# Expert sums, end norm, third norm and the second half's first products in one stage, tile by tile

## The reference, cut to what matters

```python
    h = h + hier_moe(rms_norm(h, norm2_gain[l]), ...)   # each token: two experts' rows, weighted
    return rms_norm(h, final_norm_gain)                 # "end norm"; result is x of the second half

    h = rms_norm_2(x, norm_mix_pre[l])                  # "third norm"
    c_q, c_kv, k_rope, sc_b, sc_c, sc_h, ssd_in = jnp.split(h @ w_in[l], IN_SPLITS, axis=-1)
    ...
    x = x + rms_norm_2(mixed, norm_mix_post[l])         # x is needed again here
```

## Time and profile before

| | us |
|---|---|
| median of 3 runs | 3203.65 |
| lowest and highest of them | 3199.31 and 3207.77 |
| the profiled execution, whole | 3191.12 |
| its span, first to last instruction | 3189.4 |

### The profile page before, as it was taken

The page is one execution under the profiler, slowest core; times in us unless marked ns, Lnnn a source line. Parts: engine busy times, 40 slices in busy tenths (PEclk is TensorE's granted clock), DMA queues, the critical chain, the costliest instruction groups (busy, mean ns, idle before and its releaser), DMA issues. The chain is left out here.

```text
span 3189.4 us, 39300 instructions
## 1 busy us (share of the span) xinstructions
PE 2807.9 (88%) x14664; PEld 2310.0 (72%) x14665; DVE 1757.9 (55%) x2227; ACT 1342.4 (42%) x1915; POOL 405.5 (13%) x387
## 2 busy tenths in 40 slices
PE   7999799989967299999993699679989999998997
PEld 6988577777856078888882588457768888887886
DVE  4441276777643389999995412766665334433313
ACT  4111255555531077777873423334444323322212
POOL 0000064556510200000002000220000000000000
PEclk9999899999978699999996799889999999999998
DMA  7543200010051589999984201000041111110113
GB/s 252 194 174 126 103 27 33 33 65 25 8 171 60 175 328 412 408 411 407 405 365 185 75 27 39 18 1 1 0 161 52 46 46 52 46 46 27 50 49 140
DMA packets 173926, 418.23 MB, mean 131 GB/s; under 512 B 28604, under 2 KB 116592, under 8 KB 160496
## 3 DMA queue, kind: packets, MB, share of 16 engines
q1 hardware_dynamic: 158688, 362.59, 30.7%
q0 software_dynamic: 9360, 33.04, 2.6%
q10 hardware_dynamic: 5760, 20.97, 1.6%
HBM read 347.85 MB, written 68.72 MB: 131 GB/s over the span
## 5 line engine op out<-in xcount | busy, mean ns | idle before, releaser
L134 PE MATMUL psum<-part,ffn_up_w_high 128*128 128x512 f32 x704 | 277.8, 395 | 0.7 <-DVE low L3357 0.7
L136 PE MATMUL psum<-part,ffn_up_w_low 128*128 128x512 f32 x704 | 276.1, 392 | 0.0
L135 PE MATMUL psum<-low,ffn_up_w_high 128*128 128x512 f32 x704 | 273.5, 389 | 0.0
L3371 DVE SCALAR_TENSOR_TENSOR ffn_up_acc<-psum,ffn_up_taps,ffn_up_acc 128x1023 f32<-128x1023 f32 x88 | 112.8, 1282 | 285.4 <-ACT ffn_up_acc L3292 279.6
L134 PE MATMUL psum<-part,expert_x_high 128*128 128x512 f32 x512 | 206.6, 403 | 2.9 <-issue 1.5
L134 PE MATMUL psum<-project_w_high,high 128*128 128x448 f32 (+1 forms) x512 | 196.8, 384 | 13.0 <-DVE project_w_low L129 9.0
L136 PE MATMUL psum<-part,expert_x_low 128*128 128x512 f32 x512 | 203.4, 397 | 0.0
L135 PE MATMUL psum<-project_w_low,high 128*128 128x448 f32 (+1 forms) x512 | 195.4, 382 | 0.0
L136 PE MATMUL psum<-project_w_high,low 128*128 128x448 f32 (+1 forms) x512 | 195.3, 381 | 0.0
L3292 ACT ACTIVATE ffn_up_acc<-psum,ffn_up_taps 128x1024 f32<-128x1024 f32 x44 | 53.2, 1208 | 333.9 <-PE psum L136 333.9
L1080 POOL TENSOR_TENSOR mix_ab_step<-mix_abrb,mix_pair_mask 128x512 f32<-128x512 f32 x80 | 115.1, 1463 | 420.9 <-ACT mix_abrb L1193 420.5
(11 more groups left out here) (575 smaller groups left out, 6957.5 us busy)
## 6 DMA issues: line engine op xcount, KB each, us to landing
expert_gate<-in_w_gate_dram SPq DMA_DIRECT2D x32, 2048.0 KB, 10.0
expert_up<-in_w_up_dram SPq DMA_DIRECT2D x32, 2048.0 KB, 10.0
expert_down<-in_w_down_dram SPq DMA_DIRECT2D x32, 2048.0 KB, 10.8
ffn_up_w<-in_ffn_w_up_dram SPq DMA_DIRECT2D x44, 512.0 KB, 3.8
y_rows<-expert_y ACTq DMA_DIRECT2D x32, 512.0 KB, 10.8
ffn_down_w<-in_ffn_w_down_dram SPq DMA_DIRECT2D x44, 256.0 KB, 2.6
project_w<-in_w_in_dram SPq DMA_DIRECT2D x4, 2048.0 KB, 10.3
ret_feat<-project_out SPq DMA_DIRECT2D x4, 2048.0 KB, 10.1
```

The costliest lines, as they stand in the source:

```text
L134: pe.matmul(out, left[0], right[0], start=start, stop=False)
L135: pe.matmul(out, left[0], right[1], start=False, stop=False)
L136: return pe.matmul(out, left[1], right[0], start=False, stop=stop)
L3371: v.scalar_tensor_tensor(out=acc[c][u][:, i:], in0=wide(psum, 4 * u + 2 * c, 2)[:, 0:S - i], scalar=taps[:, last_tap - i, ds(at, 1)], in1= ...
```

## The change

`combine_stage` and `norm_stage` go, and `project2_stage` takes in their work. Tile `t` is gathered, summed, multiplied by the end gain (`weighed`), squared twice (the sum, and the weighed sum), scaled once by both norms' factors and both gains (`xs`), turned, split and multiplied. The factors of both norms come from one chain of small operations on two numbers a row (`means`, `root`, `scale`). POOL makes the rows of `x2_rows` (weighed rows by the end norm's factor), and SP stores them. The gathers have two buffers in place of eight, the products three pairs of banks in place of four, the other pair takes the transposes. The gain of the third norm is now a row (a multiplication on DVE before the transpose), so the high part and the rest are each written in two pieces of 128 x 512. The first two loads of `w_fm` and their splits stand apart from the loop.

```diff
-                combine_stage(nc, x, squares, y_rows, slot_index, slot_weight, a["final_norm_gain"], x2_dram)
-            norm_stage(nc, "norm3", bank, ident, x, squares, a["norm_mix_pre_2"], part, low=low)
+        def tm_bank(t, n):
+            return bank[2 * (t % 3) + n]
...
+            gather(0)
+            gather(1)
+            for t in range(TT):
+                if t + 2 < TT:
+                    pool.wait_ge(summed, 2 * t + 2)
+                    gather(t + 2)
+                pool.wait_ge(xs_ready, t + 1)
+                pool.tensor_scalar(weighed[t % 2][:], weighed[t % 2][:], x_stats[:, t, 3, 0:1], None, ALU.mult).then_inc(x_ready, 1)
         @block.sync
+            sp.dma_start(end_gain[:], rows(a["final_norm_gain"], D)).then_inc(end_gain_loaded, 16)
+            sp.dma_start(gain[:], rows(a["norm_mix_pre_2"], D)).then_inc(gain_loaded, 16)
...
+            for u, at in enumerate((SC_AT, XBC_AT)):
+                load_fm(0, u, at)
+            for t in range(TT):
+                sp.wait_ge(x_ready, t + 1)
+                sp.dma_start(x_dram[t * P:(t + 1) * P, :], weighed[t % 2][:]).then_inc(x_stored[t % 2], 16)
         @block.tensor
+            turn(0)
             for t in range(TT):
-                tile = slice(t * P, (t + 1) * P)
-                if t >= 4:
-                    pe.wait_ge(latent_out, t - 3)
-                    pe.wait_ge(z_out, t - 3)
+                pe.wait_ge(feat_low_out, 2 * t + 2)
+                if t >= 3:
+                    pe.wait_ge(latent_out, t - 2)
+                    pe.wait_ge(z_out, t - 2)
                 for n, (lo_, hi) in enumerate(((0, LATENT), (LATENT, TM_COLS))):
+                    if n and t + 1 < TT:
+                        turn(t + 1)
...
         @block.scalar
+            def square_sum(t):
+                act.wait_ge(summed, 2 * t + 2)
+                if t:
+                    act.wait_ge(squared, 2 * t)
+                act.activation(acc[:], x[:, t, :], ACT.Square, accum_out=x_stats[:, t, 0, 0:1]).then_inc(squared, 1)
...
+            def take_high(t):
+                act.wait_ge(turned, t + 1)
+                for h in range(2):
+                    split_high(act, tile(high, t)[:, 4 * h:4 * h + 4, :], three(bank[6 + h][:], 4)).then_inc(feat_high_out, 1)
...
+            split_tm(0)
+            square_sum(0)
+            square_weighed(0)
+            split_tm(1)
+            root(0)
+            split_tm(2)
+            split_tm(3)
+            take_high(0)
+            square_sum(1)
+            square_weighed(1)
+            split_tm(PIECES)
+            root(1)
+            for t in range(TT):
+                if t + 2 < TT:
+                    square_sum(t + 2)
+                if t + 1 < TT:
+                    take_high(t + 1)
+                if t + 2 < TT:
+                    square_weighed(t + 2)
+                take_latent(t)
+                if t + 2 < TT:
+                    root(t + 2)
+                if t == TT - 3:
+                    for u in range(2):
+                        split(0, u)
...
         @block.vector
+            def add(t):
+                v.wait_ge(gathered[t % 2], t // 2 * 32 + 32)
+                for c in range(2):
+                    if c:
+                        v.wait_ge(summed, 2 * t + 1)
+                    v.scalar_tensor_tensor(out=x[:, t, :], in0=got[t % 2][:, c, :], scalar=slot_weight[:, c, t:t + 1],
+                                           in1=x[:, t, :], op0=ALU.mult, op1=ALU.add).then_inc(summed, 1)
+            def weigh(t):
+                v.wait_ge(summed, 2 * t + 2)
+                if t >= 2:
+                    v.wait_ge(x_stored[t % 2], t // 2 * 16)
+                v.tensor_tensor(weighed[t % 2][:], x[:, t, :], end_gain[:], ALU.mult).then_inc(weighed_ready, 1)
+            def means(t):
+                v.wait_ge(squared, 2 * t + 2)
+                v.tensor_scalar(x_stats[:, t, 1, 0:1], x_stats[:, t, 0, 0:1], 1.0 / D, EPS, ALU.mult, ALU.add).then_inc(stats_order, 1)
+                v.wait_ge(stats_order, t * 4 + 1)
+                v.reciprocal(x_stats[:, t, 3, 0:1], x_stats[:, t, 1, 0:1]).then_inc(stats_order, 1)
+                v.wait_ge(stats_order, t * 4 + 2)
+                v.tensor_tensor(x_stats[:, t, 3, 1:2], x_stats[:, t, 0, 1:2], x_stats[:, t, 3, 0:1], ALU.mult).then_inc(stats_order, 1)
+                v.wait_ge(stats_order, t * 4 + 3)
+                v.tensor_scalar(x_stats[:, t, 1, 1:2], x_stats[:, t, 3, 1:2], 1.0 / D, EPS, ALU.mult, ALU.add).then_inc(mean_ready, 1)
+            def scale(t):
+                v.wait_ge(root_ready, t + 1)
+                v.reciprocal(x_stats[:, t, 3, :], x_stats[:, t, 2, :]).then_inc(stats_order, 1)
+                v.wait_ge(stats_order, t * 4 + 4)
+                v.tensor_tensor(x_stats[:, t, 2, 0:1], x_stats[:, t, 3, 0:1], x_stats[:, t, 3, 1:2], ALU.mult).then_inc(both_ready, 1)
+                v.wait_ge(both_ready, t + 1)
+                if t >= 2:
+                    v.wait_ge(turned, t - 1)
+                v.scalar_tensor_tensor(out=xs[t % 2][:], in0=weighed[t % 2][:], scalar=x_stats[:, t, 2, 0:1], in1=gain[:],
+                                       op0=ALU.mult, op1=ALU.mult).then_inc(xs_ready, 1)
+            def take_low(t):
+                for h in range(2):
+                    v.wait_ge(feat_high_out, 2 * t + h + 1)
+                    split_low(v, tile(low, t)[:, 4 * h:4 * h + 4, :], three(bank[6 + h][:], 4), tile(high, t)[:, 4 * h:4 * h + 4, :])\
+                        .then_inc(feat_low_out, 1)
...
+            add(0)
+            v.wait_ge(end_gain_loaded, 16)
+            weigh(0)
+            split_tm(0)
+            means(0)
+            split_tm(1)
+            v.wait_ge(gain_loaded, 16)
+            scale(0)
+            add(1)
+            weigh(1)
+            split_tm(2)
+            split_tm(3)
+            take_low(0)
+            means(1)
+            split_tm(PIECES)
+            scale(1)
             for t in range(TT):
-                v.wait_ge(product, 2 * t + 2)
-                v.tensor_copy(rows2[:, t, LATENT:], bank[2 * (t % 4) + 1][:, 0:SSD + SSD_HEADS]).then_inc(z_out, 1)
+                if t + 2 < TT:
+                    add(t + 2)
+                    weigh(t + 2)
+                if t + 1 < TT:
+                    take_low(t + 1)
+                if t + 2 < TT:
+                    means(t + 2)
+                take_z(t)
+                if t + 2 < TT:
+                    scale(t + 2)
+                if t == TT - 3:
+                    for u in range(2):
+                        split(0, u)
```

More of the change, by code:

```diff
@@ L143, in square_rows @@
     act.activation(junk[t % 2][:], x[:, t, :], ACT.Square, accum_out=squares[:, t:t + 1]).then_inc(done, 1)
[L146 to L240, removed]
@@ L2265, in _ @@
             each_more(v, more_block)
[L2268 to L2316, removed]
-                    v.scalar_tensor_tensor(out=x[:, t, :], in0=x[:, t, :], scalar=rstd[:, t:t + 1], in1=gain[:], op0=ALU.mult,
-                                           op1=ALU.mult).then_inc(normed, 1)
-        @block.scalar
-        def _(act):
-            for g in range(TT // GROUP):
-                for t in range(g * GROUP, (g + 1) * GROUP):
-                    act.wait_ge(added, 2 * t + 2)
-                    if t >= 2:
-                        act.wait_ge(squared, t - 1)
-                    act.activation(junk[t % 2][:], x[:, t, :], ACT.Square, accum_out=square[:, t:t + 1]).then_inc(squared, 1)
-                act.wait_ge(mean_ready, g + 1)
-                act.activation(root[:, g * GROUP:(g + 1) * GROUP], mean[:, g * GROUP:(g + 1) * GROUP], ACT.Sqrt).then_inc(root_ready, 1)
-            act.wait_ge(squared, TT)
-            for t in range(TT):
-                act.wait_ge(normed, t + 1)
-                square_rows(act, x, t, junk, squares, x_squared)
@@ L2462, in scale_first, with split_tm, square_weighed, root @@
                     .then_inc(sc_scaled, 1)
-            for n, (ks, ns) in enumerate(tm_parts):
+            def split_tm(n):
+                ks, ns = tm_parts[n]
                 act.wait_ge(tm_loaded[n], 32 if n == PIECES else 16)
                 split_high(act, w_tm_high[:, ks, ns], w_tm[:, ks, ns]).then_inc(tm_high_ready, 1)
-            for u in range(2):
-                split(0, u)
-            for t in range(TT):
+            def square_sum(t):
[3 more added lines that the diff above has]
+                act.activation(acc[:], x[:, t, :], ACT.Square, accum_out=x_stats[:, t, 0, 0:1]).then_inc(squared, 1)
+            def square_weighed(t):
+                act.wait_ge(weighed_ready, t + 1)
+                act.wait_ge(squared, 2 * t + 1)
+                act.activation(acc[:], weighed[t % 2][:], ACT.Square, accum_out=x_stats[:, t, 0, 1:2]).then_inc(squared, 1)
+            def root(t):
+                act.wait_ge(mean_ready, t + 1)
+                act.activation(x_stats[:, t, 2, :], x_stats[:, t, 1, :], ACT.Sqrt).then_inc(root_ready, 1)
```

(15 more changed lines are left out.)

57 lines of the change are left out of this document (43 added, 14 removed).

## The result

| | before | after |
|---|---|---|
| median | 3201.48 us (4 runs, 3190.55 to 3207.77) | 3154.67 us (4 runs, 3149.01 to 3165.87) |
| span of the profiled execution | 3189.4 | 3158.4 |
| the stage (see below) | 147.4 | 102.6 |

The ratio is 0.9862, with a 95% interval from 0.9819 to 0.9904: 46.8 us less on the medians, where 46 were forecast.

A forecast was written before the change was run, and what follows sets the result against it. Vector engines and DMA bound the first part, PE the rest, one behind the other. Overlapped, start, 9.5 us periods and PE's tail end at 1814.1 instead of 1861.0: 46.9 saved, rounded to 46, giving 3157.7 us, range 3143 to 3180.

The forecast's parts named there:

- The bound before, and the form of the gain: Experts' end to loop of 512: vector engines and DMA bound until 1796.5 us, then PE; overlapping hides the smaller part.
- The period: Steady state, add to add: one chain over DVE and ACT, 9.10 us plus hand-overs, taken as 9.5 us a tile.
- hand-overs: Steady-state passes between engines: seven at 0.03 us give 9.3 a tile, at 0.1 as upper bound 9.8; 9.5 taken.
- Which chain: Steady state: add, squares, take_high, take_latent, root and scale set the period; PE's 8.7 us fit below, pausing 0.8 a tile.
- the other branch is shorter: Steady state: the path through weigh, take_low, means and take_z is shorter, as DVE does these while ACT squares.
- The start: Stage's first tiles: first add at 1723.7 us, between 1721.7 and 1726.4; xs(0) at 1732.7, add(2) at 1744.8.
- The end: Last tiles: add(7) at 1792.3 us, take_low(6) ends 5.7 later, then PE sets the time until 1814.1.
- Costed at nothing: Whole stage: POOL's x2 rows (1.0 to 2.9 us), gathers, SP's issues (free near 1730) and late splits, all covered.
- Rival A: Start: taps and dt columns crowd DMA, xs(1) late by some 10 us; saved 36 us; chance 0.09.
- Rival B: Steady state: POOL's rows slow DVE's rows by 30%, period 1.5 us longer; saved 37 us; chance 0.08.
- Rival C: Steady state: products and chain wait for each other, period 15.1 us; saved 18 us; chance 0.05.
- D: PE's products: pauses and transposes hold the lower clock, 16.8 us a tile; end 11 us later, 3215 us; chance 0.03.

The follow-up runs named there:

- e1: Changed kernel with the overlap undone: all tiles normed and turned first, then PE's products, with latents and z in later loops; stage 153.8 us, whole 3209.7 us.
- e3: Changed kernel with the root ahead of take_latent in ACT's order; period 9.17 us, stage 100.5 us, whole 3152.4 us.
- e4: Changed kernel with x2 rows on ACT and the root ahead of take_latent; period 8.43 us, stage 96.2 us, ratio to the kernel before 0.9828.
- e9: Changed kernel with one more wait on POOL, so its row runs after DVE's next weighing; period 8.77 us, stage 98.1 us, whole 3137.3 us.
- e6: Changed kernel with SP holding back dt columns, taps and what stands behind them until tile 0's rows came; first add 11.3 us, stage 102.4 us.
- e5: Changed kernel with SP holding back second gain, weights and small loads until tile 0's rows came; first add 8.0 us, stage 103.7 us.
- e2: Changed kernel with the x2 rows made on ACT in place of POOL; period 8.77 us, stage 97.9 us, whole 3154.8 us.
- e8: Changed kernel measured again, unchanged; stage 102.2 us, whole 3159.4 us, ratio to the kernel before 0.9885.
- e7: e4 with a new start: loads held until tile 0's rows came, root table early, tile 0's norm ahead of weight splits; stage 93.7 us, ratio 0.9849.

## Why the prediction was right, point by point

- **The bound before, and the form of the gain: right and shown.** The prediction had PE's products and the vector work of a tile overlap, with the smaller hidden under the larger. e1 undoes just that and loses 51.2 us.
- **The period: 9.5 forecast, 9.52 measured, by terms that cancel.** By starting times in the timelines above, the steps are: add 3.37 (forecast 2.63), square 1.07 (1.16), high part 0.95 (1.16), second square 1.04 (1.16), latents to root 1.26 (1.14), root to reciprocal 0.23 (0.21), scale to next add 1.60 (1.64). The add was 0.74 too cheap, as what POOL's row does to it was costed at nothing. ACT's first three steps were 0.42 too dear, since the next instruction starts before the last one's ends in the record. The 0.4 that I added for hand-overs was not needed as such; it stood in for the net 0.42 of these terms. That the sum came within 0.02 us is luck, the chain that it adds up is not.
- **Which chain: right.** That ACT's take_latent stands in it is shown by e3, and that PE was about 1 us a tile from being the bound, by its wait of 0.95 and by e4 (9.52 to 8.43). That "the other branch is shorter" was right but by little: 0.35 us, as e3 and e1 show. The step left out was that the means and take_z come on the chain as soon as take_latent goes.
- **The start: right in kind, mis-sized.** First add 9.9 us after the stage's start forecast (1723.7), 11.5 measured, within the bounds of 7.9 and 12.6 from the earlier trace rows. add(2) at 31.0 forecast, 32.6 measured: the whole 1.6 is the first add's. Between the two 21.1 were forecast and 21.2 measured, again by terms that cancel, as add(1) too ran beside a row of POOL (3.34 us) and the splits and small operations after it were cheaper than costed. The choice "nearer the first end, as both queues share" was wrong, as the truth was nearer the other.
- **The end: right.** Stage without the last copy 100.3 forecast, 102.6 measured; 1.7 of the 2.3 is there when add(7) starts. The other 0.6 lies in the tail, where take_low(6) ended 6.3 us after the start of add(7) in place of 5.7, the add being dearer there too. PE's 16.1 us from there are as forecast.
- **Costed at nothing: the cover held, two prices did not.** POOL's row took 3.82 us, above my upper bound of 2.9, which I had from twice a row of 512; it took 2.85 in e9. SP was free only at 1749.6, 25.5 us after its first issue and not 16: the dt columns alone took 7.73 us to issue. The first store left then, and nothing waited for it: DVE's weigh of tile 2 followed its add at once.
- **Rival A (crowded DMA): in part.** The first add was late by 3.6 us against the kernel before, not by 10 on top. e6 clears the small elements; e5 shows that the gain and the weights do it.
- **Rival B (POOL against DVE): in part, and the one I should have weighed more.** Of DVE's operations only the second of the two summing ones paid, 2.03 us in place of 1.28. That is 0.74 us a tile, of which six tiles' worth or 4.4 us reached the stage, not 9. The Trainium skill (GPSIMD Engine Reference, Specifications) tells of contention when a DVE instruction has two SBUF inputs. By e2 and e9 that holds here for this operation; the first summing one, the weighing and the splits of `w_fm`, which have two SBUF inputs as well, were not slowed (see the last section). My reason against it, four adds in 5.29 us beside gathers, was about descriptors and not about a row operation on POOL.
- **Rival C (no overlap) and D (clock held low): refuted.** The period was 9.52 and not 15.1. The clock was 1.00 from 1756.64 on, with a pause of 0.95 to 1.0 us in five of the tiles. The case that the Trainium skill describes (TensorE: Matmul & The Clock Gate, A second HAM failure mode: psum-queue depth-cycling), a clock that goes to and fro with short pauses between groups of products, did not occur. In e1, where PE made transposes alone, the clock stayed at 0.50 for 59.5 us. One reading of mine was off: over the old transposes have a mean of 0.56, not 0.50 throughout.
- **The whole.** 46 forecast (46.9 by the stage, rounded down), 46.8 on the medians, 44.8 in the stage. The stage is the better measure, and by it the forecast was 2.1 us too high. That the medians meet the 46 so closely is luck: the two sets of the changed kernel alone have medians 4.7 us apart (3154.67 and, in e8, 3159.37).

## What to carry to other kernels

When stages with different bounds are merged tile by tile, write the chain down step by step over all in-order queues, and then look for the second longest branch as well: it limits what any mending brings. An operation that is hidden in time may still slow the one that hides it, so place it beside work that it doesn't slow (here DVE's splits from PSUM); one more wait can be enough for that. And ahead of each wait for a late load, ask what stands behind it in that queue.

## What the runs showed of the hardware that I had not expected

- POOL's row of 1024 (one tensor input) took 3.82 us beside the summing operations of DVE and 2.85 when it ran beside splits from PSUM (e9). In the changed kernel the last such row, beside two splits of DVE with both inputs in SBUF, took 4.81 (timelines of POOL, then DVE):

```profile
1813.91 4.81 POOL L2264 TENSOR_SCALAR weighed<-weighed,project_x_stats 128x1024 f32<-128x1024 f32 x1 [5.69 <-DVE project_xs L2494]
```

```profile
1813.73 2.35 DVE L129 TENSOR_TENSOR project_w_fm_low<-project_w_fm,project_w_fm_high 128x1024 fp32r<-128x1024 f32 x2
```

  DVE's two splits took 1.22 us each all the same, as in e2 without a row on POOL (1.22). Of the two summing operations the first, which began 0.18 us before POOL's row, took 1.28 as without it, and the second, which began while the row ran, 2.03. The weighing behind them took its usual 1.22 to 1.23, though it began 0.6 us before the row's end. So what decides is not the number of SBUF inputs alone. That the operation which starts first keeps its speed would fit the first summing operation, but no run tried it. POOL paid in both cases.
- Issuing the dt columns, a load of 16-byte pieces, took SP 7.3 to 8.0 us in the kernels that issue it right behind the weights, 3.95 in e5, 1.29 in e7, and 0.52 for the same load in e6, after tile 0 had landed. The DMA share was 1.01 over the 7.73 us of the changed kernel, and 1.00 over the 0.52 us of e6, so busy DMA engines are not the whole reason. It is open.
